# Products of a constant tile in TensorE's waits, and gates that alternate with retention scores

## What is computed

```python
def trunk(x, ...):
    for layer in range(2):
        if layer == 0:
            mix = even_mixer(x)     # p = x @ ev_w_in; retention with head norm and silu gate; S5 scan,
                                    # y -> z = gelu(y), z * sigmoid(z @ s5_w_glu + b); concat @ ev_w_out
        else:
            mix = odd_mixer(x)      # p = x @ od_w_in; wkv7 over time; latent attention over the paged
                                    # cache for the samples; concat @ od_w_out
        x = layer_norm(ALPHA * x + mix, ln1)
        x = layer_norm(ALPHA * x + hier_moe(x), ln2)

def hier_moe(x):   # 16 experts in 4 groups: one group by argmax, the two best experts in it
    y = sum over the chosen experts of (silu(x @ w_gate) * (x @ w_up)) * weight @ w_down
```

## Time and profile before

| | us |
|---|---|
| median of 3 runs | 954.78 |
| lowest to highest | 954.42 to 955.5 |
| span of the profiled execution | 955.4 |
| TensorE matmul busy | 859.7 (90%) |
| DVE busy | 437.2 (46%) |
| ScalarE busy | 248.5 (26%) |
| GpSimd busy | 165.2 (17%) |
| mean granted TensorE clock | 0.896 of full speed |

### The profile page before, as it was taken

One profiled execution on the slowest core, in us unless ns is written; L12 is line 12 of the kernel. 1 busy time (PEld: TensorE's weight loads), 2 busy tenths in 40 slices (PEclk: granted clock), 3 DMA queues, 4 the chain that ended last, 5 costly groups with the idle time before them and its releaser, 6 DMA issues.

```text
span 955.4 us, 20686 instructions
## 1 busy us (share of the span) xinstructions
PE 859.7 (90%) x8588; PEld 620.0 (65%) x8588; DVE 437.2 (46%) x963; ACT 248.5 (26%) x542; POOL 165.2 (17%) x217
## 2 busy tenths in 40 slices
PE   5999898978999998999879788898998969999994
PEld 3787776756556565877655666667765757566653
DVE  3599754753124236047824343424454453042435
ACT  1135213043010114154434222121470070101013
POOL 5106042001400001000049830002610002200000
PEclk9999979987899999999999776755799977999997
DMA  9764802252999994432010130002626355999901
GB/s 266 259 175 74 163 12 94 89 220 87 400 415 417 413 338 140 149 97 69 2 18 4 60 110 3 3 1 71 187 88 221 132 225 195 417 416 417 408 20 46
DMA packets 79835, 165.25 MB, mean 173 GB/s; under 512 B 19809, under 2 KB 58136, under 8 KB 70850
## 3 DMA queue, kind: packets, MB, share of 16 engines
q1 hardware_dynamic: 68348, 149.43, 43.7%
q0 software_dynamic: 6624, 14.06, 5.1%
q10 hardware_dynamic: 4768, 0.41, 0.4%
HBM read 155.70 MB, written 6.99 MB: 170 GB/s over the span
## 4 chain that ended last, share of the span: by engine, by line
PE 78%; DVE 11%; ACT 5%; issue 3%; SPq 2%; DMA 1%; DVEq 0%; ACTq 0%
PE bank L1676 12%; PE bank L2103 12%; PE bank L1972 7%; PE bank L2135 7%; PE bank L2147 5%; PE bank L822 3%; DVE scratch L2221 3%; PE bank L676 2%; SPq L2928 1%; PE bank L926 1%; PE bank L2092 1%; PE bank L2082 1%; PE bank L700 1%; PE bank L2071 1%; DVE scratch L2218 1%
## 5 line engine op out<-in xcount | busy, mean ns | idle before, releaser
L2682 ACT ACTIVATE scratch<-bank 128x280 f32<-128x280 f32 (+6 forms) x125 | 58.1, 474 | 421.8 <-PE bank L2135 115.4
L1676 PE MATMUL bank<-x_fm,weight_slots 128*128 128x280 f32 x576 | 142.7, 409 | 2.7 <-ACT x_fm L2780 1.3
L1676 PEld LDWEIGHTS bank<-x_fm,weight_slots 128*128 128x128 f32 x576 | 111.8, 195 | 31.5 <-issue 3.5
L2103 PE MATMUL bank<-weight_slots,scratch 128*64 128x256 f32 x672 | 94.1, 385 | 0.0
L2221 DVE TENSOR_TENSOR scratch<-bank,scratch 128x256 f32<-128x256 f32 x16 | 6.8, 425 | 158.5 <-PE bank L2103 158.5
L2103 PEld LDWEIGHTS bank<-weight_slots,scratch 128*64 128x64 f32 x672 | 59.2, 139 | 27.1 <-issue 5.9
L2147 PE MATMUL bank<-scratch 128*128 128x280 f32 x256 | 66.6, 406 | 0.0
L2221 DVE TENSOR_TENSOR scratch<-scratch 128x128 f32<-128x128 f32 (+14 forms) x76 | 50.8, 682 | 30.3 <-ACT scratch L2682 28.4
L1972 PE MATMUL bank<-scratch,weight_slots 128*128 128x280 f32 x256 | 64.2, 410 | 0.0
L1972 PEld LDWEIGHTS bank<-scratch,weight_slots 128*128 128x128 f32 x256 | 49.2, 194 | 13.9 <-issue 1.3
L2103 PE MATMUL bank<-scratch 128*64 128x256 f32 x352 | 56.9, 379 | 0.0
(11 more groups left out here) (450 smaller groups left out, 1310.8 us busy)
## 6 DMA issues: line engine op xcount, KB each, us to landing
weight_slots<-in_moe_w_down SPq DMA_DIRECT2D x24, 1024.0 KB, 11.1
weight_slots<-in_moe_w_up SPq DMA_DIRECT2D x22, 1024.0 KB, 9.4
weight_slots<-in_moe_w_gate SPq DMA_DIRECT2D x20, 1024.0 KB, 10.1
scratch<-in_moe_w_gate SPq DMA_DIRECT2D x12, 1024.0 KB, 8.9
scratch<-in_moe_w_up SPq DMA_DIRECT2D x10, 1024.0 KB, 10.2
weight_slots<-in_od_w_in SPq DMA_DIRECT2D x9, 1024.0 KB, 5.8
weight_slots<-in_ev_w_in SPq DMA_DIRECT2D x8, 1024.0 KB, 14.4
scratch<-in_moe_w_down SPq DMA_DIRECT2D x8, 1024.0 KB, 11.5
```

Source lines behind the costliest of these rows:

```text
L1676: ins = pe.matmul(b[:, 0:NT], w[:, k, P * m2:P * m2 + P], src[:, k, :], start=(k == 0), stop=(k == kt - 1))
L2103: ins = pe.matmul(b[CAP * j:CAP * j + CAP, 0:DE], XG[:, q % 2, k, CAP * j:CAP * j + CAP], w[j][:, k, :], start=(k == 0), stop=(k == KD - 1))
L2682: return act.activation(dst, b[:rows, 0:width], f, **kw).then_inc(ring.free, 1)
```

## The change

On TensorE, `keep(b, n)` issues n products of a constant tile of zeros, 32x32 by 32x256, into bank b. The bank's real products start with `start=True` and overwrite them. The tile is written once by DVE at the beginning. Calls stand ahead of the wait for the input (13), the S5 input transposes (2 and 1), the injection (1), in the end of the even mixer (4 times 1, 3 times 2, and 3), ahead of the head norm's sums (3), and for each layer ahead of the norm's scale (1), the router's scale (1), `x_turned` (8), `pack(0, 0)` (7), the first `down` (3); ahead of layer norm 2's scale (3 in layer 0, 5 in layer 1), of the first projection of the odd mixer (3) and of the output rows (5). For this the claims of the banks move ahead of the waits. The four gate products alternate with the four heads' scores. DVE makes `PARTO` before its product for the gate, not after it. The 16 rope pages of four samples share one event.

```diff
@@ -249,6 +249,7 @@
...
         S = sb("scratch", [P, SCRATCH])
+        WARM = sb("warm", [32, 288])
@@ -527,7 +528,7 @@
...
-        def odd_pe(pe, ln_tile, V, A, close, until, slot, used, to_fm, project, fm_sums, out_and_moe):
+        def odd_pe(pe, ln_tile, keep, V, A, close, until, slot, used, to_fm, project, fm_sums, out_and_moe):
@@ -920,7 +921,8 @@
...
                         pe.wait_ge(ev(f"cache_kv_in{sm}_{half}"), 16 * 4)
-                        pe.wait_ge(ev(f"cache_krope_in{sm}_{half}"), 16 * 4)
+                        if j == 0:
+                            pe.wait_ge(ev(f"cache_krope_in{g}_{half}"), 16 * 16)
@@ -997,12 +999,14 @@
...
+            first = V.claim()
+            keep(first, 5)
...
                 for t, (c0, r) in enumerate(TT):
-                    b = V.claim()
+                    b = first if h == t == 0 else V.claim()
@@ -1574,7 +1578,7 @@
...
                     page.append(pool.value_load(PTAB[0:1, i:i + 1], min_val=0, max_val=a["cache_krope"].shape[0] - 1))
-                pool.dma_start(CK[sm, pg][:, 256:288], a["cache_krope"][bass.ds(page[n], 1), 0].rearrange("o p c -> p (o c)")).then_inc(ev(f"cache_krope_in{sm}_{pg // 4}"), 16)
+                pool.dma_start(CK[sm, pg][:, 256:288], a["cache_krope"][bass.ds(page[n], 1), 0].rearrange("o p c -> p (o c)")).then_inc(ev(f"cache_krope_in{sm // 4}_{pg // 4}"), 16)
@@ -1644,6 +1648,11 @@
...
+            def keep(b, n):
...
+                for _ in range(n):
+                    pe.matmul(b[0:32, 0:256], WARM[:, 0:32], WARM[:, 32:288], start=True, stop=True)
@@ -1655,6 +1664,10 @@
...
                     b = V.claim()
+                    if m == 0:
+                        pe.wait_ge(ev("warm_set"), 1)
+                        keep(b, 13)
+                        pe.wait_ge(ev("x_in"), 16 * len(x_loads))
@@ -1666,10 +1679,13 @@
...
-            def project(n, m2, width, src, kt, ring, name, ready=None):
...
-                b = ring.claim()
+            def project(n, m2, width, src, kt, ring, name, ready=None, b=None):
...
+                if b is None:
+                    b = ring.claim()
                 w = slot_view(n, kt, width)
+                if ready:
+                    keep(b, 3)
@@ -1677,7 +1693,6 @@
...
-            pe.wait_ge(ev("x_in"), 16 * len(x_loads))
@@ -1727,8 +1742,10 @@
...
             for q in range(4):
+                b = A.claim()
+                if q > 1:
+                    keep(b, 4 - q)
                 pe.wait_ge(ev("ucq_ready"), q + 1)
-                b = A.claim()
@@ -1739,10 +1756,13 @@
...
             until("bit")
+            b = A.claim()
+            keep(b, 1)
...
                 for h in range(2):
-                    b = A.claim()
+                    if j or h:
+                        b = A.claim()
@@ -1825,29 +1845,32 @@
...
             until("y_chunk")
+            glu0 = A.claim()
...
                 close(V, ins, "y_fm")
+                keep(glu0, 1)
             for t, (c0, r) in enumerate(TT):
+                keep(glu0, 2)
...
+            keep(glu0, 3)
+            slot(S_GLU)
...
-            slot(S_GLU)
-            pe.wait_ge(ev("z_ready"), 1)
-            for m in range(4):
-                project(S_GLU, m, 512, ZF, 4, A, "glu")
+                if h == 0:
+                    pe.wait_ge(ev("z_ready"), 1)
+                project(S_GLU, h, 512, ZF, 4, A, "glu", b=glu0 if h == 0 else None)
@@ -1890,10 +1913,11 @@
...
-            def spread_scale(c):
...
+            def spread_scale(c, n):
...
+                b = V.claim()
+                keep(b, n)
                 pe.wait_ge(ev("ln_scaled"), (KD + 1) * c + 1)
-                b = V.claim()
@@ -2019,26 +2044,29 @@
...
                 close(A, ins, f"lg{l}")
-                spread_scale(2 * l)
...
-                def x_turned(t):
+                spread_scale(2 * l, 1)
...
+                def x_turned(t, first=None):
...
                     for h in range(2):
-                        b = A.claim()
+                        b = first if first is not None and h == 0 else A.claim()
...
+                b = V.claim()
+                keep(b, 1)
                 pe.wait_ge(ev("lg_scaled"), l + 1)
-                b = V.claim()
...
                 close(V, ins)
+                first = A.claim()
+                keep(first, 8)
...
                 for t in range(3):
-                    x_turned(t)
+                    x_turned(t, first if t == 0 else None)
@@ -2059,8 +2087,9 @@
...
                     if half == 0:
+                        xg[q] = [V.claim() for c in range(4)]
+                        keep(xg[q][0], 7)
                         pe.wait_ge(ev("dispatch_ready"), NG * l + q // 2 + 1)
-                        xg[q] = [V.claim() for c in range(4)]
@@ -2125,9 +2154,12 @@
...
                     w = [slot_view(n + j, 2, D) for j in range(2)]
-                    until(f"ht{l}")
...
                         b = G.claim()
+                        if h == 0:
+                            if q == 0:
+                                keep(b, 3)
+                            until(f"ht{l}")
@@ -2197,16 +2229,17 @@
...
                     close(V, ins, "prev")
-                spread_scale(2 * l + 1)
+                spread_scale(2 * l + 1, 3 if l == 0 else 5)
...
             out_and_moe(0, S_EVO)
-            odd_pe(pe, ln_tile, V, A, close, until, slot, used, to_fm, project, fm_sums, out_and_moe)
+            odd_pe(pe, ln_tile, keep, V, A, close, until, slot, used, to_fm, project, fm_sums, out_and_moe)
...
             s = Steps(dve, dve_step)
+            dve.memset(WARM[:, :], 0.0).then_inc(ev("warm_set"), 1)
@@ -2418,11 +2451,11 @@
...
+            dve.wait_ge(ev("read_out"), 1)
+            s.do(dve.tensor_reduce(PARTO, TOUT.rearrange("p d v -> p v d"), AX.X, ALU.add), ev("parto_ready"))
...
-            dve.wait_ge(ev("read_out"), 1)
-            s.do(dve.tensor_reduce(PARTO, TOUT.rearrange("p d v -> p v d"), AX.X, ALU.add), ev("parto_ready"))
...
             b = V.take()
```

## The result

The changed kernel takes 980.46 us (median of 4 runs, 977.38 to 984.34) against 955.0 us in 4 runs of the kernel before beside it: a ratio of 1.029 (95% interval 1.026 to 1.033). It is slower by 2.9%, where 940 was forecast. The profiled execution has a span of 977.8 us against 955.4, so 22.4 us are to be found. What the prediction drew up as the rival "Slower" came.

A forecast was written before the change was run, and what follows sets the result against it. TensorE, holding 78% of the chain, bounds the kernel, its clock often low behind waits or sparse work. Gains at the filled places, less 0.3 for the rope event, sum to 15.4 us off 955.4: 940, range 930 to 953.

The forecast's parts named there:

- rival "Slower": Whole kernel: a 32x32 tile doesn't lift or hold the clock; about 35 us lost, 990; chance 0.12, with milder forms.
- The price of one product: Each keep product, two instructions: 0.43 us at full clock, 0.86 at half; 89 added, 38 us at full clock.
- give back the clock if such a small tile counts as activity: All fills: products free while ending ahead of their wait, returning the clock if 32x32 counts; rows 8 as evidence.
- Start, 4.7: Thirteen products before the input lands; gain cut to 4.7 us by DVE's s5_rows chain; bounds 4.7 and -2.3.
- S5 input, 0.7: Products (2, 1, 1) roughly fit the waits; 3.4 us at half clock; gain 0.7, at most 1.2, other end -0.3.
- End of the mixer, 2.9: Even mixer's end: thirteen products let scores and gate run at full clock; gain 2.9, bounds -3 to 3.3; alternation worth little.
- Packing: Seven products ahead of pack, layer 0: pack starts 1.8 to 4.7 us after its slots, halves at full clock; gain 0.3.
- Norm and first odd projection 1.4: After layer 0's norm, 3 + 3 products fill waits of 1.5 and 1.3 us; gain 1.4, ScalarE's tiles binding.
- Head norm 1.5: 1.3 us of products in a wait of 1.7 ahead of half-clock projection products; gain 1.5, bounds -0.9 to 1.7.
- Layer 0, 2.4: From x_turned to down, fills (1, 1, 8, 7, 3): 0.3 + 0.8 + 1.3 = 2.4 us gain, bounds -3 and 7.
- Layer 1, 1.3: Same places as layer 0; first gates already at full clock can lose; gain 1.3, bounds -4 and 6.
- The rival "transposes let the clock fall": After the fills, transposes drop the clock; x_turned and output rows give nothing; gain 11, or 944; chance 0.08.

The follow-up runs named there:

- e1: The changed kernel with the keep tile made full, 128x128 by 128x256, still zeros: 943.59 us, ratio 0.989.
- e2: As e1, but the full tile filled with 0.7 in place of zeros: 945.68 us, ratio 0.990.
- e3: The changed kernel with its 32x32 tile filled with 0.7 in place of zeros: 982.39 us, ratio 1.030.
- e9: The changed kernel with a stationary tile of 128 rows by 32 columns of zeros: 946.38 us, ratio 0.992.
- e10: The changed kernel with a stationary tile of 32 rows by 128 columns of zeros: 980.61 us, ratio 1.028.
- e5: e1 without the fills at the mixer's end (13), ahead of pack (7) and of the first down (3): 942.64 us, ratio 0.988.
- e7: e5 with eight products ahead of pack, written to a bank of ring A before ring V's claims: 940.29 us, ratio 0.987.
- e12: e7 without the thirteen products at the start: 939.49 us, ratio 0.985.
- e13: e11 with 15 products at the start in place of 13: 938.05 us, ratio 0.984.
- e6: e5 without the thirteen products at the start: 940.15 us, ratio 0.985.
- e8: The kernel before with only the alternation of gate products and head scores: 949.32 us, ratio 0.996.
- e15: Control: e11 without any product at the start: 938.99 us, ratio 0.985.
- e11: e7 with the second half of projection 1 moved ahead of the transposes that wait for in_s_c_re: 941.18 us, ratio 0.985.

## Why the prediction failed, point by point

**The price of one product: right.** 0.43 us per instruction at half clock (11.29 us for 26) and 0.215 at full clock.

**The step that failed: the fills "give back the clock if such a small tile counts as activity".** The 32x32 tile didn't: the first 26 instructions stay 0.43 apart for 11.3 us, and the same kernel with all 128 rows fed (e1) halves that from 7.5 us on and is 37 us faster. The assumption rested on rows 8, 130 instructions on 32x32 tiles in a stretch at full clock, and the text itself called them evidence and no proof, because other tiles were busy beside them. They were no evidence: these tiles are busy for 1.53 of 3.40 us there. A view of the kernel before has the same line in another stretch, and that row, which the prediction doesn't show, speaks the other way:

```profile
655.00:658.40 3.40, 2.83 (x86) 2.51 (x87) 0.50 0.79 213
```

There line 822 is all that TensorE does (tiles of 16x16), for 2.83 of 3.40 us, and the clock is at 0.50. It is no proof either, since the clock was already low when the stretch began; but the two rows side by side would have made the rival likelier than 0.12. e1, e2, e3, e9 and e10 decide it. Every gain in the sum hung on this one step, and it was given 0.88. The rival's own sign, the first transposes past 12 us at 0.28 each, came to the digit (12.57, 0.285). Its terms for the two layers (9 each) came near, 7.8 and 8.3; of 35 us 22 came. Norms, ends and the S5 input cost 0.9 in all and not 6, the mixer 7.1 and not 9 (the alternation, worth 2.4 to 3.1 by itself, is the likely reason, not isolated here), and 3.9 came back in the odd mixer.

**Start, 4.7: right in size up to 31.9 us with a full tile, wrong in what is late next.** e1 had 4.50 there. The forecast said `s5_rows` on DVE would be late next; it was, by 0.56 us, and behind it stood a transfer that lands at 30.8. The chain of before shows no trace of it, because there TensorE came at 32.2. Its landing should have been looked up: each wait between the gain and the end of the stretch ends at a time of its own, which a faster TensorE runs into.

**S5 input, 0.7: mis-sized.** 2.7 to 3.0 with a full tile in e1, e2, e5 and e7, 0.5 without fills. In e1 1.5 of them come by 82 us, where the clock was held, twice the term; the other 1.6 come at 109.6 us, where the wait for a transfer ahead of L1782 is 0.98 us and was 2.56. What made that transfer earlier isn't traced.

**End of the mixer, 2.9: wrong, in both halves.** With a full tile the products cost 7.2 us (5.4 ahead of L1837 and 1.8 ahead of L1844), since the clock fell behind the first of them (0.50 from 126.8 to 133.6 us), and 5.3 came back behind them. The forecast took the clock to stay up there. It also has a slip: 5.6 us of products less 1.6 hidden put the scores at 137.6, not at 136.8. The alternation alone gave 2.4 to 3.1, where nothing was booked.

**Packing: the lateness came, a little over its bound.** 1.8 to 4.7 us behind the slots was said, for the claims on the ring; it was 5.1 in the changed kernel and 5.2 with the full tile. e7 shows that without the claims it can be 0.8, e12 that it is 4.0 even so where the clock is low when the products begin.

**Norm and first odd projection 1.4: right** with a full tile (1.4, and 0.0 without fills). Output rows 0.8: near, 1.2 at the end, with DVE's evictions binding as said. Head norm 1.5: 1.7 with a full tile, but 1.7 in the changed kernel too, so the fill isn't shown to be its cause. Layer 0, 2.4: 0.9 with the fills as changed and a full tile, 4.8 in e7; but 3.3 with no fill at all. Layer 1, 1.3: 1.0 and 2.3, against 2.8 with no fill. The rope event, 0.3: 0.0 between 685 and 700 us.

**Sum.** With the assumption made true (e1) the span is 944.0, 11.4 us less than 955.4; the forecast said 15.4. But 4.5 of e1's come from the odd mixer, by luck of the execution, and about 7 from the stretches that the change touches. The forecast took 1.9 us for what a measurement tells from no change; the kernel before alone ran from 948.1 to 957.1 us. It also counted eight stretches at half clock outside the odd mixer's long cold part, where the trace has four more (231.8, 245.4, 784.7 and 941.7 us).

**The rival "transposes let the clock fall".** Of eight executions with a full-height fill at the start, three lost the clock during the 24 transposes or right behind them (at 12.9, 12.8 and 15.8 us), those in which it had risen earliest (6.1, 5.9 and 5.5 us); in five it held through them into the projection (rise at 6.4 to 7.5). Short waits for the input ahead of the transposes don't sort them: 0.4, 1.0 and 0 us in the three, 0 to 0.5 in the five. So the clock held through the same transposes in some executions and not in others. The Trainium skill, page "TensorE: Matmul & The Clock Gate", Part 4 on the PE-mode transpose, says that they don't count as busy in the same way; the three fit it, the five don't show it. That they are the cause isn't isolated here.

## What to carry to other kernels

Before filling waits with dummy products, measure one: put a dozen at the very start and see whether their spacing halves. Feed all 128 rows; zeros will do. Then fill only waits that the products fit at the half-clock price (e12 paid it: the packing 4.0 us late), claim nothing for them on which the wait itself depends, and look up when every transfer behind the gain lands. Before a gain is put down to a fill, look at the same stretch in a kernel without it. Real products of 128 rows set in among those of 64 cost nothing, and gave 2.4 to 3.1 us here, about as much as the best fill (2.7 to 3.0 at the S5 input, 0.5 of it without).

## What the hardware did that was not expected

- In these runs the fed rows made the difference, not the busy time. TensorE stays at 1.2 GHz while it is busy for 17.10 of 17.10 us with 32-row tiles between transposes, and with scores of 64 rows and gate products at the end; in the start's thirteen products the clock rises at 6.4 us with 128x32, with 32x128 not at all. That the 64-row scores of the even mixer run cold for the same reason is argued from this, not shown.
- It rises on zeros as on the value 0.7: at 7.4 and 6.1 us, 943.6 and 945.7 us in all.
- The same start fill saw the rise at 5.5 to 7.5 us in different executions. The Trainium skill, page "TensorE: Matmul & The Clock Gate", Part 1 on the clock gate, says that this moment differs from run to run, by about 0.5 us either way. The runs agree that it differs, but they spread over 2.0 us. The three earliest rises are those whose clock fell again in or behind the transposes.
- The odd mixer, in which no instruction changed but a wait for the rope pages, moved by -4.6 to +1.8 us among the profiled executions of the table and by -7.5 (e10) to +6.6 (e13) among all, and between 724 and 766 us several (e2, e5, e6, e7, e8, e13, e15) lose 5.0 us that others keep. The kernel before ran from 948.1 to 957.1 us in the four later batches against 954.4 to 955.5 in its first four runs. Differences of 1 to 2 us in this kernel need more runs than were made here, which is why e5, e6, e7, e11, e12, e13 and e15 (938.1 to 942.6) are not ranked.
